# Fifteen extra products on the matrix engine while a mixture-of-experts routing waits

## What is computed

```python
def moe_swiglu(x, w_router, b_router, w_g, w_u, w_d):
    logits = (x @ w_router).astype(jnp.float32) + b_router.astype(jnp.float32)
    top_v, top_i = lax.top_k(logits, TOP_K)
    top_w = jax.nn.softmax(top_v, axis=-1)
    combine = jnp.sum(jax.nn.one_hot(top_i, N_EXPERTS, dtype=jnp.float32) * top_w[..., None], axis=-2)
    ...
    for e in range(N_EXPERTS):
        y = y + combine[..., e:e + 1] * swiglu(x, w_g[e], w_u[e], w_d[e])
    return y
```

## Time and profile before

| | |
|---|---|
| device time, median of 3 runs | 1679.0 us (1677.57, 1679.0, 1679.09) |
| the profiled execution's own time | 1678.43 us |
| its span, first to last instruction | 1676.6 us |
| mean granted TensorE clock | 0.984 |
| busy: PE / DVE / ACT / POOL | 95% / 69% / 49% / 11% |
| routing and item 0, by the products' times | from 1039.84 us to 1121.9 us of the span |

### The profile page before, as it was taken

One profiled execution on the slowest core, in us unless ns is written; L12 is line 12 of the kernel. 1 busy time (PEld: TensorE's weight loads), 2 busy tenths in 40 slices (PEclk: granted clock), 3 DMA queues, 4 the chain that ended last, 5 costly groups with the idle time before them and its releaser, 6 DMA issues.

```text
span 1676.6 us, 20036 instructions
## 1 busy us (share of the span) xinstructions
PE 1584.8 (95%) x7315; PEld 1261.0 (75%) x7315; DVE 1156.1 (69%) x1312; ACT 813.8 (49%) x1093; POOL 177.5 (11%) x115
## 2 busy tenths in 40 slices
PE   7999999999999999999999999789999999999990
PEld 6877778888888888788777787667777777777770
DVE  6888747594444423478886676788877788877776
ACT  5344442252222211343443424567777777777771
POOL 0410006060000000005000150200000000000006
PEclk9999999999999999999999999899999999999995
DMA  5232232325544333223222333779999999999994
GB/s 207 76 101 75 66 111 89 101 76 201 176 169 145 125 101 95 69 91 98 76 75 76 104 113 137 283 268 356 383 355 353 355 358 355 387 353 353 352 344 163
DMA packets 134380, 325.69 MB, mean 194 GB/s; under 512 B 7984, under 2 KB 19632, under 8 KB 133808
## 3 DMA queue, kind: packets, MB, share of 16 engines
q1 hardware_dynamic: 125440, 291.32, 49.6%
q0 software_dynamic: 5440, 20.97, 3.2%
q10 hardware_dynamic: 3440, 12.58, 1.9%
HBM read 300.20 MB, written 24.64 MB: 194 GB/s over the span
## 4 chain that ended last, share of the span: by engine, by line
PE 72%; DMA 13%; DVE 6%; ACT 4%; issue 4%; ACTq 0%; SPq 0%; POOL 0%; DVEq 0%
PE bank L1292 15%; PE bank L1293 14%; PE bank L1294 14%; DMA eraw<-expert_gu 11%; PE bank L1331 4%; PE bank L1330 4%; PE bank L1332 4%; PE bank L1573 3%; PE bank L1575 3%; PE bank L1574 3%; ACT ewhi L697 3%; PE bank L1580 2%; DVE ewlo L1025 2%; PE bank L1404 1%; PE bank L1417 1%
## 5 line engine op out<-in xcount | busy, mean ns | idle before, releaser
L1025 DVE TENSOR_TENSOR ewlo<-eraw,ewhi 128x2048 fp32r<-128x2048 f32 x168 | 383.9, 2290 | 95.6 <-ACT ewhi L697 95.0
L1292 PE MATMUL bank<-xth,whi 128*128 128x512 f32 (+1 forms) x976 | 381.1, 390 | 2.9 <-DVE wlo L801 2.9
L801 DVE TENSOR_TENSOR wlo<-raw,whi 128x1024 fp32r<-128x1024 f32 x170 | 239.7, 1413 | 206.1 <-ACT whi L502 205.7
L1293 PE MATMUL bank<-xtl,whi 128*128 128x512 f32 (+1 forms) x976 | 370.3, 379 | 0.0
L1294 PE MATMUL bank<-xth,wlo 128*128 128x512 f32 (+1 forms) x976 | 370.1, 379 | 0.0
L697 ACT ACTIVATE ewhi<-eraw 128x2048 fp32r<-128x2048 f32 x168 | 321.6, 1915 | 93.1 <-DMA eraw<-expert_gu 57.9
L502 ACT ACTIVATE whi<-raw 128x1024 fp32r<-128x1024 f32 x170 | 178.5, 1051 | 137.0 <-PE bank L1332 123.9
L1292 PEld LDWEIGHTS bank<-xth,whi 128*128 128x128 f32 x976 | 183.5, 188 | 52.2 <-issue 8.5
L1573 PE MATMUL bank<-ewhi,xgh 128*128 128x512 f32 (+1 forms) x528 | 206.1, 390 | 6.4 <-DVE xgl L1092 4.9
L1293 PEld LDWEIGHTS bank<-xtl,whi 128*128 128x128 f32 x976 | 183.7, 188 | 36.7 <-issue 3.8
L1294 PEld LDWEIGHTS bank<-xth,wlo 128*128 128x128 f32 x976 | 183.6, 188 | 35.1
(11 more groups left out here) (233 smaller groups left out, 2086.0 us busy)
## 6 DMA issues: line engine op xcount, KB each, us to landing
eraw<-expert_gu SPq DMA_DIRECT2D x124, 1024.0 KB, 9.3
raw<-dense_w SPq DMA_DIRECT2D x170, 512.0 KB, 3.5
eraw<-expert_dn SPq DMA_DIRECT2D x44, 1024.0 KB, 11.4
eraw<-expert_dn SPq DMA_DIRECT2D x22, 768.0 KB, 10.5
item_rows<-zero POOLq DMA_DIRECT2D x8, 1024.0 KB, 4.9
rows<-item_rows ACTq DMA_DIRECT2D x11, 512.0 KB, 6.5
item_results<-yrows ACTq DMA_DIRECT2D x11, 512.0 KB, 7.3
lngb<-lnrow SPq DMA_DIRECT2D x3, 1024.0 KB, 5.5
```

The source lines that it names most:

```text
L801: V.tensor_tensor(wlo[:, g % SPL, :], raw[:, g % RAW, :], whi[:, g % SPL, :], ALU.subtract).then_inc(lo_done, 1)
L1025: V.tensor_tensor(ewlo[:, o % ESPL, 0:n], eraw[:, p % ERING, 0:n], ewhi[:, o % ESPL, 0:n], ALU.subtract).then_inc(e_lo, 1)
L1292: mm(out, wh, xh, start=first, stop=False)
L1293: mm(out, wh, xl, start=False, stop=False)
```

## The change

PE gets a helper that makes float32 products of 128x128 by 128x256 constants (`ident` and the first 256 columns of `cst`) into bank 7, which is not read between the logits and the first item's second block of hidden features. They stand at three places: four ahead of the wait for `rt_both`, two ahead of the waits for `xr_lo` and `rt_sel`, and nine behind `turn_rows`. None of them waits for a semaphore or raises one.

```diff
             ins.then_inc(rt_turned, 1)
+
+            def keep_streaming(n):
+
+                for _i in range(n):
+                    mm(bank[7][:, 0:SEQ], ident, cst[:, 0:SEQ], start=True, stop=True)
+
+            keep_streaming(4)
             pe.wait_ge(rt_both, 1)
...
             ins.then_inc(rt_cnt, 1)
 
 
+            keep_streaming(2)
             pe.wait_ge(xr_lo, TT)
             pe.wait_ge(rt_sel, 1)
...
             pe.wait_ge(rows_own, 2)
             turn_rows()
+            keep_streaming(9)
             pe.wait_ge(rt_tab, 1)
             turns = pe.value_load(tab[0:1, 16:17], min_val=NE, max_val=MAX_ITEMS)
```

## The result

The changed kernel takes 1682.2 us against 1679.2 us (medians of twelve runs each). The ratio is 1.0019, with a 95% interval of 1.0011 to 1.0027, so the change costs 1.8 to 4.5 us. I had forecast 1677.3 us, in a range of 1674.2 to 1680.7, and no change; the median lies 1.5 us above that range, and the interval leaves out no change. The profiled execution took 1681.85 us, 3.42 more than the profiled one of before.

What follows compares the result with a forecast made beforehand. DVE was taken to bound item 0, with PE at half clock twice before and in it. 1678.43 - 2.65 - 2.56 (held clock) + 4.05 (ACT's wait for the scatters) = 1677.3 us, range 1674.2 to 1680.7.

Steps and rivals of the forecast that it cites:

- The cost of the products: In PE's three pauses at routing and gathering: 0.44 us a product at full clock, fitting the pauses, so no cost.
- What a held clock removes: At the gathering 2.65 us and at item 0's piece 0 another 2.56 us, so DVE's run starts 5.2 us sooner.
- The place where it stops: In item 0 ahead of splitting piece 6, ACT stands idle 3 to 5 us until all eight scatters have landed.
- The size of S: Landing time of the last scatter in item 0: between 1077.9 and 1079.8, middle 1078.85, for a gain of 1.1 us.
- the rival with 0.20: At item 0's scatters: DVE's low parts slow POOL's instructions by 2.4 us, landing 1080.3 or 1082.2, kernel slower; chance 0.20.
- the stop: Software queue's near halt beside expert weights, 3.5 us from 1069; moved forward whole, last landing 1079.8, gain 0.2 us.
- the half share: At item 0's scatters the software queue keeps half the engines' time beside the weights, ending at 1076.3, gain 3.6 us.
- Behind item 0 I take the shift as rigid: From about 1110.84 on, everything waits only for work of the shifted chain, so the shift is kept.
- The late gate: In item 0, scatters slowed by DVE's low parts land at 1080.3 or 1082.2; 1678.4 to 1680.7 us, chance 0.20.
- The early gate: In item 0 the software queue keeps its half and the scatters land early; 1673.2 to 1676 us, chance 0.20.
- no effect on the clock: PE's clock falls in routing and item 0 despite the products; 1678.4 us if they still fit, chance 0.05.
- an overrun of the products: At half clock the products outlast PE's routing and gathering pauses, PE 4.5 us late; 1682.9 us, chance 0.07.

Runs made afterwards that it cites:

- experiment 3: The changed kernel with its fifteen products cut from 256 columns to 8; 1678.9 us, 1.0003 of the kernel before.
- experiment 1: The changed kernel with the load of the next item's rows and ACT's scatter wait moved from ahead of split 6 to ahead of split 10; 1675.1 us, ratio 0.9975.
- experiment 8: The kernel before, with two more DVE subtractions of a low part's size right behind the row numbers; 1681.8 us, ratio 1.0012.
- experiment 4: The changed kernel with only the first six products (four and two), without the nine behind the turned rows; 1680.6 us, ratio 1.0006 to the kernel before.
- experiment 7: The changed kernel with SP waiting for all scatters before it loads the weights of piece 7; 1680.0 us, ratio 1.0005 to the kernel before.
- experiment 5: The kernel before, with the rows' load and ACT's scatter wait moved from ahead of split 6 to ahead of split 4; 1689.8 us, ratio 1.0060.
- experiment 6: The changed kernel with only the nine products behind the turned rows; 1679.9 us, ratio 0.9998 to the kernel before.
- experiment 2: The kernel before, with the rows' load and ACT's scatter wait moved from ahead of split 6 to ahead of split 10; 1679.4 us, ratio 1.0003.

## Why the prediction was wrong, step by step

**The cost of the products: right.** 0.22 us a pass, all three groups end 0.3 to 0.9 us ahead of need, and experiment 3 prices the bare instructions at nothing.

**What a held clock removes: right.** Forecast 2.65 + 2.56 us, measured 2.51 us at the gathering and, with piece 0, 5.13 us at low part 3. One row was misread without harm to the sum: 1071.05 in the earlier trace rows is the end of piece 0's last product, and the next piece's first stands at 1070.85. Experiment 1 shows that this reaches the end when nothing takes it back: item 1's first product stands at 1117.63 there, and at 1121.34 before. The logits of that execution started 0.97 us late (1040.81), so the gain there is 4.7 us.

**The place where it stops: right.** ACT waits for the scatters ahead of split 6, for 6.36 us where I had said 3 to 5.

**The size of S: this step failed.** The prediction said that S lies between 1077.9 and 1079.8 and to "take the middle, 1078.85". In the frame of before the last scatter landed at 1080.4, beyond both ends, and a gain of 1.1 us became a loss of 0.6. The bounds let only the expert weights act on S. What was left out of them stood in the trace of before, in the earlier trace rows, and in the rival with 0.20: POOL's instructions are slowed by DVE's low parts. That rival gave 2.4 us on 1077.9, S = 1080.3. Its mechanism is what happened; that the number fits so well is partly luck, since the instructions delayed the last start by 2.8 us, and from there the landing took 9.0 us instead of 9.4. Experiments 8 and 4 show the cause: 1.9 to 2.9 us for an instruction that starts beside a low part, 0.95 for one that doesn't. The sooner DVE's run starts, the more scatters lie beside it. The engine that was to be sped up delays the very event that it then waits for.

My doubt about that rival drew on the Trainium skill (SBUF — State Buffer, Who interferes with whom), which infers that making descriptors isn't hit by a DVE instruction with two SBUF inputs. These scatters were hit: 0.95 us became 1.90 and 2.86, and the measurement decides. Whether it is the making of descriptors that is held up, or the reading of the row numbers (`ridx`), which the same section would let such a DVE instruction hold up, no run separates. My other ground for doubt, that the eighth scatter stayed slow when DVE had stopped, was half a misreading: it began at 1068.51, and DVE's low parts ran until 1069.58. In experiment 4, where the last two scatters begin behind DVE's end, they take 0.95 us.

The refills do have the effect that I named, at the other end: 9.0 us from start to landing with them, 5.1 without (experiment 7). But this was so before as well, with 9.4; the stop did not grow longer when it moved forward. In the changed kernel the software queue had 10.6% of the engines' time from 1069 to 1072, when the weights had 79.5%, and between 36% and 70% in the stretches after. So neither the stop moved whole nor the half share held throughout.

**"Behind item 0 I take the shift as rigid": wrong inside item 0.** Behind it the shift is rigid: from item 1's first product to the end of the span it is 555.4 us, and 555.3 before. But between low part 6 and the second low part of item 1 the delay grew from 0.57 to 1.98 us. These are the rows of before for low parts 6 and 9 and that of item 1; the changed kernel's are 1084.25, 1093.62 and 1124.35:

```profile
1082.47 2.29 DVE L1025 TENSOR_TENSOR ewlo<-eraw,ewhi 128x2048 fp32r<-128x2048 f32 x1
...
1091.03 2.29 DVE L1025 TENSOR_TENSOR ewlo<-eraw,ewhi 128x2048 fp32r<-128x2048 f32 x1 [0.29 <-ACT ewhi L697]
...
1121.16 2.29 DVE L1025 TENSOR_TENSOR ewlo<-eraw,ewhi 128x2048 fp32r<-128x2048 f32 x1 [1.42 <-ACT ewhi L697]
```

With the gate PE runs dry, for 5.20 us, and the clock that the products had held falls there. Piece 6 takes 4.54 us (1086.60 to 1091.14) instead of 2.88; ACT waits 3.03 us for what follows it, and low part 9 waits 1.22 us for ACT. That is 0.81 us. The second fall, at 1107, delays piece 13, which frees the slot for the weights of item 1's second piece, and that piece's low part comes another 0.61 us later ([2.02 <-ACT], ACT [2.19 <-DMA]). I had priced the clock in the pauses that I saw, and not in the pause that I predicted.

That the fall at piece 6 follows from the gate is borne out by experiment 1, where piece 6 takes 2.88 us again with the wait gone, and by experiment 5, where a gate in another place brings a fall of its own. Where the pause behind the gate was short, 1.16 us in experiment 4 and 0.59 in experiment 8, the clock did not fall there.

The second fall does not need the gate. It comes behind a pause of PE ahead of piece 11, which the kernel before has as well; first before, then the changed kernel:

```profile
1103.42 0.43 PE L1552 MATMUL bank<-cst,eh 128*128 128x128 f32 x2 [1.86 <-DVE eh L1115]
```

```profile
1106.00 0.43 PE L1561 MATMUL bank<-cst,eh 128*128 128x128 f32 x2 [1.86 <-DVE eh L1115]
```

All ten traces have this pause, with 1.79 to 1.88 us. Behind it the clock fell for 3.41 us in five (the changed kernel and experiments 1, 4, 6 and 8, the last without any product) and stayed at 1.00 in the other five. Why it falls in some stays open. Its price is borne out: from low part 9 to the second low part of item 1 the delay grows by 0.68 to 0.76 us in experiments 1, 4 and 8 (and by 1.97 in 6, where I don't know what else came in), against 0.04 to 0.13 in experiments 2, 3, 5 and 7, where the clock held.

**The sum, mended.** 1678.43 - 5.13 (held clock) + 5.70 (taken back at the gate, 0.57 late) + 0.81 + 0.61 (the clock in item 0) = 1680.4, and with the 1.21 of the late start 1681.6 against 1681.85. Without the late start this is 2.0 us of loss, inside the interval of 1.8 to 4.5; the remaining microsecond between it and the medians I can't place. Of the 2.0 us, 0.61 hang on the second fall, which kernels with and without the products show in some traces and not in others.

**The rivals.** The late gate came true in its mechanism and its S. Its price had the gate alone: 1678.8 for S = 1080.3, and 1680.7 for a landing at 1082.2 that did not come. The two falls of the clock in item 0 added 1.4 us. The early gate, no effect on the clock and an overrun of the products are refuted by the rows above.

## What to carry to other kernels

When a change lets an engine start sooner, list the events that do *not* move with it, and ask two things of each: when does the sooner engine meet it, and does the sooner engine itself delay it. Holding a clock through a pause pays only if the time won isn't stood out in a new pause, where the clock is lost again; here moving one wait, which alone is worth nothing, turned 3 us of loss into 4 us of gain. A duration that doubles in two rows of a list of eight (0.95 to 1.90) belongs in the sum, and not only in a rival.

## What the runs showed of the hardware

A DVE subtraction of 128x2048 float32 with both inputs in SBUF stretches POOL's indirect DMA instructions that start beside it, from 0.95 us to 1.9 and up to 2.86 (the changed kernel, experiments 4 and 8); why some take 1.9 and others 2.8 stays open. A subtraction of 128x512 (0.69 us) beside one did not: the fourth scatter of before took 0.95 us with such a one beside it from 1062.42 on. Expert weights on the hardware queue don't stretch the instruction (2.84 and 2.68 us without them, 2.82 and 2.69 with them), but its landing, from 5 to 9 us. And the clock fell for 3.41 us behind some pauses and for 6.83 behind others: 3.41 behind 5.20 us of idle PE, 6.83 behind 3.10 in experiment 5, and behind pauses of 1.8 to 1.9 us in item 0 it fell in five traces of ten.
